# Weighted sums of a forgetting attention with the exponentials as stationary operand, on one NeuronCore

## What is computed

```python
def one_block(args):                      # 128 queries, all 16 heads of 64 channels
    logits = (jnp.einsum('bhqn,bhkn->bhqk', qb, kh).astype(jnp.float32) * scale
              + cqb[..., None] - ck[:, :, None, :])
    mask = key_pos[None, :] <= q_pos[:, None]
    logits = jnp.where(mask, logits, -jnp.inf)
    p = jax.nn.softmax(logits, axis=-1)
    return jnp.einsum('bhqk,bhkn->bhqn', p.astype(vh.dtype), vh)
...
    return h + (attn * jax.nn.silu(z)) @ w_out
```

## Time and profile before

| | |
|---|---|
| median of 3 runs | 2131.5 us (2128.23 to 2131.59) |
| profiled execution | 2133.43 us, span 2131.6 us, mean granted clock 0.966 |
| busy in the span: PE, PEld | 1964.1 us (92%), 1684.4 us (79%) |
| busy in the span: DVE, ACT, POOL | 1051.4 us (49%), 943.6 us (44%), 234.2 us (11%) |
| chain that ended last | PE 74%, DVE 9%, ACT 9%, issue 5%, DMA 2% |
| weighted sums, L2107 | 448 passes, 1309.4 to 2027.9 us |

### The profile page before, as it was taken

The page is one execution under the profiler, slowest core; times in us unless marked ns, Lnnn a source line. Parts: engine busy times, 40 slices in busy tenths (PEclk is TensorE's granted clock), DMA queues, the critical chain, the costliest instruction groups (busy, mean ns, idle before and its releaser), DMA issues.

```text
span 2131.6 us, 56907 instructions
## 1 busy us (share of the span) xinstructions
PE 1964.1 (92%) x24895; PEld 1684.4 (79%) x24895; DVE 1051.4 (49%) x1991; ACT 943.6 (44%) x1677; POOL 234.2 (11%) x261
## 2 busy tenths in 40 slices
PE   6699999999999999999889789999999999999798
PEld 4588888889898888889779577777777877777477
DVE  2646565666656665665623543343343533443521
ACT  2445454444444444454412253544555364444621
POOL 0011111111111111111000021001010101100000
PEclk9799999999999999999869898999999999999799
DMA  5101000010101000010231210010110110110233
GB/s 201 50 2 42 11 25 27 18 38 5 47 8 37 15 27 27 12 41 8 77 108 52 101 42 21 26 30 21 35 26 26 35 31 21 30 35 16 79 114 118
DMA packets 103738, 89.92 MB, mean 42 GB/s; under 512 B 4101, under 2 KB 95864, under 8 KB 103240
## 3 DMA queue, kind: packets, MB, share of 16 engines
q1 hardware_dynamic: 100120, 68.50, 10.9%
q0 software_dynamic: 3168, 17.14, 2.5%
q10 hardware_dynamic: 208, 0.66, 0.1%
HBM read 64.96 MB, written 21.33 MB: 40 GB/s over the span
## 4 chain that ended last, share of the span: by engine, by line
PE 74%; DVE 9%; ACT 9%; issue 5%; DMA 2%; SPq 0%; ACTq 0%; DVEq 0%; POOLq 0%
PE ps L1711 6%; PE ps L2024 6%; PE ps L2026 5%; PE ps L2025 5%; PE ps L1713 5%; PE ps L1712 5%; PE ps L2107 5%; PE ps L1815 4%; PE ps L1647 3%; PE ps L1649 3%; PE ps L1648 3%; PE ps L1844 2%; PE ps L2060 2%; PE ps L2088 2%; PE ps L1839 2%
## 5 line engine op out<-in xcount | busy, mean ns | idle before, releaser
L1711 PE MATMUL ps<-xh,wh 128*128 128x258 f32 (+1 forms) x1024 | 328.0, 320 | 7.5 <-ACT arena L887 3.5
L1712 PE MATMUL ps<-xh,wl 128*128 128x258 f32 (+1 forms) x1024 | 291.2, 284 | 0.0
L1713 PE MATMUL ps<-xl,wh 128*128 128x258 f32 (+1 forms) x1024 | 291.0, 284 | 0.0
L2024 PE MATMUL ps<-xh,wh 128*128 128x348 f32 x768 | 262.3, 341 | 8.4 <-ACT arena_b L1075 5.2
L2025 PE MATMUL ps<-xh,wl 128*128 128x348 f32 x768 | 248.5, 324 | 0.0
L2026 PE MATMUL ps<-xl,wh 128*128 128x348 f32 x768 | 248.3, 323 | 0.0
L1711 PEld LDWEIGHTS ps<-xh,wh 128*128 128x128 f32 x1024 | 193.6, 189 | 26.0 <-ACT arena L887 6.0
L1591 DVE TENSOR_REDUCE arena_b<-ps 128x1 f32<-128x144 f32 (+4 forms) x224 | 106.2, 505 | 192.8 <-PE ps L2064 176.3
L1712 PEld LDWEIGHTS ps<-xh,wl 128*128 128x128 f32 x1024 | 194.3, 190 | 2.6
L1713 PEld LDWEIGHTS ps<-xl,wh 128*128 128x128 f32 x1024 | 193.6, 189 | 0.0
L1075 ACT ACTIVATE arena_b<-ps 128x348 f32<-128x348 f32 x96 | 43.9, 458 | 293.8 <-PE ps L2026 293.8
(11 more groups left out here) (255 smaller groups left out, 4357.4 us busy)
## 6 DMA issues: line engine op xcount, KB each, us to landing
wr<-in_w_in SPq DMA_DIRECT2D x33, 512.0 KB, 4.1
xt_scr<-arena POOLq DMA_DIRECT2D x2, 4176.0 KB, 13.3
wr<-in_kv_w SPq DMA_DIRECT2D x16, 512.0 KB, 3.9
wr<-in_b_w_in SPq DMA_DIRECT2D x16, 512.0 KB, 3.9
arena<-xt_scr SPq DMA_DIRECT2D x8, 522.0 KB, 4.7
arena<-oa_scr SPq DMA_DIRECT2D x8, 520.0 KB, 3.7
arena<-in_x SPq DMA_DIRECT2D x8, 512.0 KB, 3.4
wr<-in_w_out SPq DMA_DIRECT2D x8, 512.0 KB, 3.8
```

The source lines that it names most:

```text
L1711: pe.matmul(bank, wh[:, j, k, :], xh[:, k, t], start=(k == 0), stop=False)
L1712: pe.matmul(bank, wl[:, j, k, :], xh[:, k, t], start=False, stop=False)
L1713: mm = pe.matmul(bank, wh[:, j, k, :], xl[:, k, t], start=False, stop=(k == KO - 1))
L2024: pe.matmul(bank[:, 0:SEG], wh[:, slot, k, :], xh[:, k, t], start=(k == 0), stop=False)
```

## The change

The operands of the weighted sums change places. A buffer `pt` gets 112 columns of zeros in front (`PZ`), so that 128 queries on a block boundary can be taken as the loaded operand also where a unit begins in the middle of a block; V moves, 65 columns wide (64 channels and one column of ones). A query half is then four blocks of 65 columns in one bank, with queries on partitions. The denominator is a column: VectorE takes its reciprocal and multiplies (one instruction for four blocks) into `on`. Once per pair, step `otr` transposes the eight blocks of `on` back to channels on partitions through the banks of the maxima; ScalarE evacuates them to `ob`, and one VectorE instruction over 128 partitions applies 0.5 and the gate. The steps `den`, the denominator copies, both activations of the reciprocal and the first scaling product go. The store is one DMA of 128 rows per pair.

```diff
@@ buffers
-        vflat = [carve_b(NT * P).rearrange("p (t x) -> p t x", t=NT) for _ in range(2)]
-        pt = [carve_b(512) for _ in range(4)]
-        ob, den = carve_b(SEQ), carve_b(SEQ)
+        VW, PZ = HD + 1, P - META
+        vflat = [carve_b(NT * VW).rearrange("p (t x) -> p t x", t=NT) for _ in range(2)]
+        rcol = carve_b(4)
+        pt = [carve_b(PZ + 512) for _ in range(4)]
+        ob, on = carve_b(SEQ), carve_b(SEQ).rearrange("p (t c) -> p t c", t=KO)
@@ order(e, more)
-                fill[0] = [("vrow", 1, 0), ("vrow", 1, 1), ("stackk", 1), ("stackq", 1)]
+                fill[0] = [("vrow", 1, 0), ("vrow", 1, 1), ("stackk", 1), ("stackq", 1), ("otr",)]
-                    fill[2] = m(2) + proj(0, 1, *m(2))
+                    fill[2] = m(2) + proj(0, 1, *m(2)) + [("gated",)]
-                    fill[6] = [("maxrow", 1)] + proj(1, 2) + [("gated", 1)]
+                    fill[6] = [("maxrow", 1)] + proj(1, 2)
@@ POOL
-            def store_ob(p, e):
-                pool.wait_ge(S.o_gated, 2 * p + e + 2)
-                pool.dma_start(ob_scr[p][head(e), :], ob[head(e), :]).then_inc(S.ob_stored, 16)
+            def store_ob(p):
+                pool.wait_ge(S.o_gated, p + 2)
+                pool.dma_start(ob_scr[p], ob).then_inc(S.ob_stored, 16)
@@ ACT
+                    elif kind == "otr" and p > 0:
+                        act.wait_ge(S.ob_free, p)
+                        for a in range(2):
+                            act.wait_ge(S.otr_done, 2 * p - 1 + a)
+                            act.activation(ob[:, a * 512:(a + 1) * 512], ps[:, B_SM[a], :], ACT.Copy).then_inc(S.otr_copied, 1)
-                            act.activation(den[b, c], ps[o, B_PV[qb_], :], ACT.Copy).then_inc(S.pv_read, 1)
@@ DVE
-                            dve.tensor_copy(ob[b, c], ps[b, B_PV[qb_], :]).then_inc(S.pv_free, 1)
+                            dve.reciprocal(rcol.unsqueeze(2), got[:, :, HD:VW]).then_inc(S.pv_recip, 1)
+                            dve.wait_ge(S.pv_recip, 4 * p + 2 * e + qb_ + 1)
+                            dve.tensor_tensor(on[:, 4 * qb_:4 * qb_ + 4, head(e)], got[:, :, 0:HD],
+                                              rcol.unsqueeze(2).to_broadcast([P, 4, HD]), ALU.mult).then_inc(S.pv_free, 1)
+                    elif kind == "gated" and p > 0:
+                        dve.wait_ge(S.otr_copied, 2 * p)
+                        dve.wait_ge(S.bz_gate, p)
+                        dve.scalar_tensor_tensor(ob, ob, 0.5, zg[:, META:T], ALU.mult, ALU.mult).then_inc(S.o_gated, 1)
@@ PE
-                            pe.matmul(ps[:, B_PV[qb_], q0 - 512 * qb_:512], vflat[e][0:n_k, kt, :],
-                                      pt[n_ % 4][0:n_k, 0:n_q], start=(kt == 0), stop=(kt == 4 * qb_ + 4),
-                                      skip_group_check=True).then_inc(S.pv_done, 1)
+                            part = q0 % P
+                            for i in range(-(-n_q // P)):
+                                b = (q0 - 512 * qb_) // P + i
+                                c0 = i * P + (0 if part else PZ)
+                                mm = pe.matmul(ps[:, B_PV[qb_], b * VW:(b + 1) * VW], pt[n_ % 4][0:n_k, c0:c0 + P],
+                                               vflat[e][0:n_k, kt, :], start=(kt == 0 and b == 0),
+                                               stop=(kt == 4 * qb_ + b + 1), skip_group_check=True)
+                            mm.then_inc(S.pv_done, 1)
+                    elif kind == "otr" and p > 0:
+                        pe.wait_ge(S.pv_free, 4 * p)
+                        pe.wait_ge(S.m_row, min(4 * p + 2, 4 * KO))
+                        for a in range(2):
+                            for t in range(4):
+                                mm = pe.transpose(ps[:, B_SM[a], t * P:(t + 1) * P], on[:, 4 * a + t, :], ident[:, :])
+                            mm.then_inc(S.otr_done, 1)
...
-            for sem in (S.pv_free, S.pv_read):
-                pe.wait_ge(sem, 4 * KO)
+            round_pe(KO, [("otr",)])
+            pe.wait_ge(S.otr_copied, 2 * KO)
```

More of the change, by code:

```diff
@@ L420, in order @@
             if e == 0:
-                fill[0] = [("vrow", 1, 0), ("vrow", 1, 1), ("stackk", 1), ("stackq", 1)]
+                fill[0] = [("vrow", 1, 0), ("vrow", 1, 1), ("stackk", 1), ("stackq", 1), ("otr",)]
                 if more:
                     fill[1] = proj(0, 0)
-                    fill[2] = m(2) + proj(0, 1, *m(2))
+                    fill[2] = m(2) + proj(0, 1, *m(2)) + [("gated",)]
                     fill[3] = m(2) + proj(0, 2, *m(2))
-                    fill[4] = ([("sumsq", 0, i) for i in range(3)] + [("den", 1), ("rsq", 0)] + m(1) + proj(1, 0, *m(2)))
+                    fill[4] = ([("sumsq", 0, i) for i in range(3)] + [("rsq", 0)] + m(1) + proj(1, 0, *m(2)))
                     fill[5] = [("norm", 0)] + m(2) + proj(1, 1, *m(1))
-                    fill[6] = [("maxrow", 1)] + proj(1, 2) + [("gated", 1)]
+                    fill[6] = [("maxrow", 1)] + proj(1, 2)
                     fill[7] = [("gate",)]
@@ L431, in order @@
                     fill[1] = [("wsplit",)]
-                    fill[2] = m(3)
+                    fill[2] = m(3) + [("gated",)]
                     fill[3] = m(3) + [("orow", 0)]
-                    fill[4] = m(3) + [("den", 1), ("orow", 1)]
-                    fill[5] = m(3) + [("gated", 1), ("orow", 2)]
+                    fill[4] = m(3) + [("orow", 1)]
+                    fill[5] = m(3) + [("orow", 2)]
                     fill[6] = m(2) + [("gate",), ("orow", 3)]
@@ L438, in order @@
             elif more:
-                fill[0] = [("sumsq", 1, i) for i in range(3)] + [("den", 0), ("rsq", 1)] + proj(2, 0) + [("stackk", 0)]
+                fill[0] = [("sumsq", 1, i) for i in range(3)] + [("rsq", 1)] + proj(2, 0) + [("stackk", 0)]
                 fill[1] = proj(2, 1) + [("norm", 1), ("stackq", 0)]
-                fill[2] = proj(2, 2) + [("gated", 0)]
+                fill[2] = proj(2, 2)
                 fill[3] = [("vrow", 0, 0), ("vrow", 0, 1)] + m(2) + proj(3, 0, *m(2))
@@ L778, in _ @@
             pool.sem_inc(S.w_scaled, 1)
-            store_ob(KO - 2, 1)
-            store_ob(KO - 1, 0)
-            store_ob(KO - 1, 1)
+            store_ob(KO - 2)
+            store_ob(KO - 1)
         @block.scalar
@@ L1103, in round_act @@
                         act.activation(brs, brs, ACT.Exp, scale=-0.5).then_inc(S.hn_rstd, 1)
[L1104 to L1108, removed]
                     elif kind == "stackk":
@@ L1159, in round_act @@
                                 act.wait_ge(S.pv_done, n_ - 3)
-                            act.activation(pt[n_ % 4][0:n_k, 0:n_q], ps[0:n_k, B_ST[i], 0:n_q], ACT.Exp,
+                            act.activation(pt[n_ % 4][0:n_k, PZ:PZ + n_q], ps[0:n_k, B_ST[i], 0:n_q], ACT.Exp,
                                            scale=SCALE).then_inc(S.p_exp, 1)
[L1162 to L1172, removed]
-                            act.activation(den[b, c], ps[o, B_PV[qb_], :], ACT.Copy).then_inc(S.pv_read, 1)
             round_act(-1, first_round(), [c_scr[0], None])
@@ L1525, in _ @@
             dve.tensor_scalar(seg3(f_in[0:H, :]), g[0:H], fb_in[0:H, :], None, ALU.add).then_inc(S.f_logit, 1)
-            dve.memset(vflat[0][:, :, HD:], 1.0).then_inc(S.setup_b, 1)
-            dve.memset(vflat[1][:, :, 0:HD], 1.0).then_inc(S.setup_b, 1)
+            for e in range(2):
+                dve.memset(vflat[e][:, :, HD:], 1.0).then_inc(S.setup_b, 1)
             dve.memset(f_b[0:H, :], 1.0).then_inc(S.setup_b, 1)
@@ L1543, in _ @@
             dve.memset(mpart, MASKED).then_inc(S.setup_b, 1)
-            dve.wait_ge(S.setup_b, 4)
+            for a in pt:
+                dve.memset(a[:, 0:PZ], 0.0).then_inc(S.setup_b, 1)
+            dve.wait_ge(S.setup_b, 8)
             dve.sem_inc(S.o_gated, 1)
@@ L2056, in round_pe @@
                                 pe.wait_ge(S.m_row, 4 * q_ + 2 * e)
+                            if e and p:
+                                pe.wait_ge(S.otr_copied, 2 * p)
                         elif i >= 2:
```

56 lines of the change are left out of this document (18 added, 38 removed).

## The result

The changed kernel takes **2158.6 us** (median of 4 runs, 2153.2 to 2161.0) against 2131.2 for the kernel before: ratio 1.0126, 95% interval [1.0110, 1.0143], so +27.4 us where +15.9 was forecast. The profiled execution has a span of 2157.2 us, 25.6 more than before.

A forecast was written before the change was run, and what follows sets the result against it. TensorE was taken to bound the kernel. From 2131.5 us, 24.1 + 7.0 - 8.4 - 9.0 + 0.6 + 1.6 = +15.9 us gave 2147 us, range 2129 to 2168.

The forecast's parts named there:

- The bound and the pace: TensorE bounds the steady pairs; in the changed weighted sums, float32 weight loads set the spacing, 0.112 us a pass.
- The hidden loads: Rival for the weighted sums: loads run wholly beside the pass before, 0.057 us a pass, time 2070 us; chance 0.05.
- the dearer ones: Rival: loads in the weighted sums cost 0.12 us a pass, no wait relieved, time 2176 us; chance 0.13.
- The weighted sums, +24.1: TensorE's 88 load-paced passes a head cost 9.86 us in place of 8.35: +24.1 us for 16 heads.
- The transposes, +7.0: New on TensorE: eight transposes back per pair, 64 at 0.109 us each, +7.0 us.
- 0.6 and 1.6: Evacuations of the transposes on the path in the last pair, +0.6 us; longer wait before the output products, +1.6 us.
- Steady relief, -8.4: Shorter TensorE waits in the steady pairs: sums of squares, V's evacuation and exponentials, together -8.4 us.
- the sums of squares: TensorE's third sum of squares waits for ScalarE; without denominator copies in seven odd halves, 4.2 us come back.
- The last pair, -9.0: Shorter waits in the last pair give 7.0 us and the half-clock stretch behind them about 2: -9.0 us.
- the 1.5 of the forecast: Forecast change from the seventh pair's gate to the first output sum: -1.5 us.
- the 15.4 of the forecast: Part of TensorE's 41 us in its six largest waits over all eight pairs that was expected to go: 15.4 us.
- the rival in which the waits dissolve: ScalarE's relief removes 30 of TensorE's 41 us of waiting; sum +1.3 us, time 2133 us; chance 0.17.

The follow-up runs named there:

- experiment 3: The kernel before without ScalarE's part of the division (copies, Ln, Exp, table loads), the gate multiplied in instead, output not normalised: 2109.5 us, ratio 0.9900.
- experiment 6: The changed kernel without the transposes back and their evacuations, output in the wrong order: 2150.7 us, ratio 1.0083.
- experiment 1: The changed kernel with V stored 104 columns wide in place of 65, the extra columns idle: 2137.0 us, ratio 1.0020.
- experiment 2: The changed kernel with only 33 of V's 65 columns streamed, output not the attention: 2170.0 us, ratio 1.0188.
- experiment 5: The changed kernel with V 80 columns wide in place of 65: 2163.1 us, ratio 1.0146.
- experiment 7: The kernel before, with VectorE taking the reciprocals of both heads of the last pair from SBUF: 2130.9 us, ratio 0.9996.
- experiment 8: The kernel before, with VectorE taking the reciprocals of only the first head of the last pair, ScalarE keeping the very last head's: 2125.7 us, ratio 0.9978.

## Why the prediction was right in sign and wrong in size

- **The bound and the pace**: right. Float32 loads of 128 columns are 0.113 us apart, so the weighted sums run at the pace of their loads. The rule of the Trainium skill, "TensorE: Matmul & The Clock Gate", section "Back-to-back issue gap", would have had 81 ns; the section names no type for this figure, and the measurement decides against it for these float32 loads. The hidden loads (0.055 us) are out, and the dearer ones (0.12) too.
- **The weighted sums, +24.1**: somewhat too large for the steady pairs. From experiment 3 to the changed kernel a pair grows by 95.6 - 92.3 = 3.3 us, 0.8 of it transposes (experiment 6); that leaves 2.5 us for two heads where 3.02 were forecast. Of the missing 0.5, shorter waits are 0.4: TensorE's idle time over six pairs falls from 15.3 to 12.9 us, nearly all of it the wait for exponentials (4.0 to 1.9). I charged the growth in full and did not say that slower sums wait less.
- **The transposes, +7.0** with 0.6 and 1.6 for their evacuation and the end: 9.2, measured 7.9 to 9.2. Right, and right that their cover in the steady pairs holds: their only wait is the 0.7 us at the very end.
- **Steady relief, -8.4**: too small. Experiment 3 gives 2.2 us a pair, about 15 over seven. I went wait by wait and asked what stands directly in front of each, and so credited nothing in the steady pairs for the wait on VectorE's row maxima (4.3 us), which hung on ScalarE through a split of weights on VectorE (experiment 3). Another 3.8 us over six pairs went from TensorE's busy time, which I had not reckoned with at all. For the sums of squares the forecast was wrong the other way, 2.6 against 4.2.
- **The last pair, -9.0**: the step that failed. The waits did go: 15.9 us between the seventh gate and the first output sum before, 5.8 after. The 4.6 and the 1.8 us of the earlier trace rows went wholly, of the 1.7 us at most 0.6 is left, and so it is with 2.7 us at 1979.41 that I had not priced. That the 1.8 hung on VectorE's scaling products fits experiment 3, which keeps these products and this wait (1.7). But this step took for granted that the half clock goes with the waits: I credited 2 us for it. That the thinner streaming could hold the clock down was half a sentence under the dearer loads, priced as half the relief, about 9 us. Experiments 1, 2 and 5 show that it is a mechanism of its own, worth 25.2 us in that stretch (144.3 against 119.1). With the clock back the stretch is 7.8 us shorter than before, more than the 1.5 of the forecast.
- **The sum**: 15.9 - 9.4 (steady pairs) + 19.0 (last stretch) + 0.2 (the two small stretches) gives 25.7, the +25.6 of the spans to rounding. The range held, 1.4 us from its upper end, because a gain and a loss that were both missed partly cancel. That is luck: with the clock back (experiment 1, 104 columns) the change costs 4 to 6 us by the ratio and by the medians, so most of the measured slowdown comes from the mechanism that the forecast left out of its sum.

22 of the 41 us of waiting went, between the 15.4 of the forecast and the 30 of the rival in which the waits dissolve.

What stays open is why the clock follows the streaming. The runs show that it changed with the number of streamed columns, at 33, 65, 80 and 104 in this one kernel, and nothing finer.

## What to carry to other kernels

Before turning a product around (making the loaded operand the moving one), count its passes and price each by the larger of its load and its streaming. Where the load is longer, some more moving columns cost next to nothing (104 in place of 65 added 0.2 us a pair here). Then look at TensorE's granted clock in the stretch with the least other work: a change that removes its waits can still lose there, and padding the moving operand won back 21.6 us here. When pricing a wait, follow it back through the other engines' queues and not only to the instruction in front. Before ScalarE is relieved by VectorE, look at what is queued behind the new instruction: experiments 7 and 8 differ by one placement, and only the second gains.

## What the runs showed of the hardware that was not expected

- TensorE's being busy did not decide its clock here. With 65 or 80 streamed columns a load it was busy 95% of 71 and 67 us in the last pair and granted 0.50 throughout; with 104 it was granted 1.00 after 7 us; with 33 it fell to 0.50 for 3 to 7 us at a time in steady pairs, with no wait near.
- At 0.50 the spacing of full float32 loads is about 0.21 us (estimated from 16 in 3.51), twice the 0.113 at 1.00: the pace of loads followed the granted clock.
- VectorE's reciprocal costs 3.36 us for 64x512, from PSUM and from SBUF alike (3355 ns and 3.35 us), 4.9 times a copy.
